# Sums of squares between the stages of a decoder trunk: VectorE adds the tiles and TensorE sums one

## What is computed

```python
def rmsnorm(x, g):
    xf = x.astype(jnp.float32)
    y = xf * lax.rsqrt(jnp.mean(xf * xf, axis=-1, keepdims=True) + EPS)
    return (y * g.astype(jnp.float32)).astype(x.dtype)
...
        hp = hp + rmsnorm(yp, g_post_mix[i])          # yp: the token mixer of rmsnorm(hp, g_pre_mix[i])
        fp, cvp = conv_ffn(rmsnorm(hp, g_pre_ffn[i]), ffn_w_up[i], ffn_conv_w[i], ffn_conv_b[i], ffn_w_down[i], ...)
        hp = hp + rmsnorm(fp, g_post_ffn[i])
        hp = hp + ple_term(hp, p_prompt[i], g_ple[i], ple_w_gate[i], ple_w_proj[i])
```

## Time and profile before

| what | before |
|---|---|
| device time, median of 3 runs | 1294.07 us |
| the profiled execution's own time | 1293.96 us |
| its span, first to last instruction | 1292.2 us |
| TensorE matmul busy | 1283.7 us (99%) |
| TensorE weight load busy | 1251.8 us (97%) |
| VectorE busy | 877.2 us (68%) |
| ScalarE busy | 593.1 us (46%) |
| GpSimd busy | 74.8 us (6%) |
| granted TensorE clock | 1.000 of full speed |

### The profile page before, as it was taken

How to read it: one execution, slowest core, us unless ns; L and a number is a source line. 1 busy time by engine, 2 the same in 40 slices (tenths; PEclk the granted TensorE clock), 3 DMA queues, 4 the chain that set the end, 5 groups by cost and what they waited for, 6 DMA issues and landing times.

```text
span 1292.2 us, 25278 instructions
## 1 busy us (share of the span) xinstructions
PE 1283.7 (99%) x10762; PEld 1251.8 (97%) x10762; DVE 877.2 (68%) x1656; ACT 593.1 (46%) x1060; POOL 74.8 (6%) x114
## 2 busy tenths in 40 slices
PE   9999999999999999999999999999999999999998
PEld 8999989999999999999999977999999999999998
DVE  7899776887777774223896788688777777422375
ACT  6214565544444443223755777554444444222371
POOL 1112230000100000000031020000000000000000
PEclk9999999999999999999999999999999999999999
DMA  5435621213342233222314232311332323322231
GB/s 197 155 102 192 201 98 51 99 66 104 96 107 85 96 106 119 90 90 78 132 53 159 66 99 81 115 50 52 96 94 87 98 84 109 114 90 91 78 131 67
DMA packets 35617, 131.85 MB, mean 102 GB/s; under 512 B 4516, under 2 KB 5260, under 8 KB 35184
## 3 DMA queue, kind: packets, MB, share of 16 engines
q1 hardware_dynamic: 29664, 111.33, 27.0%
q0 software_dynamic: 5408, 18.26, 4.4%
q10 hardware_dynamic: 432, 0.64, 0.2%
HBM read 121.26 MB, written 10.08 MB: 102 GB/s over the span
## 4 chain that ended last, share of the span: by engine, by line
PE 98%; DVE 1%; ACT 0%; DMA 0%; issue 0%; ACTq 0%; DVEq 0%
PE tile L1171 24%; PE tile L1175 24%; PE tile L1173 24%; PE tile L1181 5%; PE tile L1182 5%; PE tile L1183 5%; PE side L1181 1%; PE side L1182 1%; PE side L1183 1%; PE tile L1643 1%; PE side L1666 1%; PE sums L1220 0%; DMA raw<-in_w_kv 0%; PE sums L1681 0%; PE sums L1342 0%; PE sums L1688 0%
## 5 line engine op out<-in xcount | busy, mean ns | idle before, releaser
L749 ACT ACTIVATE wH<-raw 128x1024 fp32r<-128x1024 f32 (+1 forms) x190 | 211.0, 1114 | 384.9 <-DMA raw<-in_w_up 150.8
L1171 PE MATMUL tile<-xH,wH 128*128 128x260 f32 x1798 | 362.5, 283 | 0.0
L1175 PE MATMUL tile<-xH,wL 128*128 128x260 f32 x1798 | 362.4, 283 | 0.0
L1173 PE MATMUL tile<-xL,wH 128*128 128x260 f32 x1798 | 361.8, 283 | 0.0
L1813 DVE TENSOR_TENSOR wL<-raw,wH 128x1024 fp32r<-128x1024 f32 (+1 forms) x190 | 245.3, 1292 | 154.4 <-ACT wH L749 150.3
L1171 PEld LDWEIGHTS tile<-xH,wH 128*128 128x128 f32 x1798 | 277.1, 188 | 3.0 <-issue 3.0
L1175 PEld LDWEIGHTS tile<-xH,wL 128*128 128x128 f32 x1798 | 277.2, 188 | 0.0
L1173 PEld LDWEIGHTS tile<-xL,wH 128*128 128x128 f32 x1798 | 276.4, 188 | 0.0
L1873 DVE SCALAR_TENSOR_TENSOR u<-tile,rstd 128x520 f32<-128x520 f32 x96 | 67.1, 699 | 121.6 <-PE tile L1175 121.6
L1171 PE MATMUL tile<-hidH,wH 128*128 128x260 f32 x616 | 124.3, 283 | 0.0
L1175 PE MATMUL tile<-hidH,wL 128*128 128x260 f32 x616 | 123.8, 282 | 0.0
(11 more groups left out here) (434 smaller groups left out, 1878.7 us busy)
## 6 DMA issues: line engine op xcount, KB each, us to landing
raw<-in_w_up SPq DMA_DIRECT2D x88, 512.0 KB, 3.6
raw<-in_w_down SPq DMA_DIRECT2D x32, 704.0 KB, 4.1
raw<-in_w_ple SPq DMA_DIRECT2D x16, 512.0 KB, 6.5
raw<-in_w_qo SPq DMA_DIRECT2D x12, 512.0 KB, 3.7
raw<-in_w_qkv SPq DMA_DIRECT2D x12, 512.0 KB, 3.6
raw<-in_w_kv SPq DMA_DIRECT2D x10, 512.0 KB, 3.7
cring<-in_c_in POOLq DMA_DIRECT2D x8, 512.0 KB, 4.8
out_c_s<-cring POOLq DMA_DIRECT2D x8, 512.0 KB, 3.1
```

The lines of the kernel that those rows point to most:

```text
L749: nc.scalar.activation(wH[j][:, 0:n], raw[j][:, 0:n], ACT.Copy).then_inc(s_high, 1)
L1171: nc.tensor.matmul(out[:, q, 0:HT], wh, x[0][:, k, tokens(q)], start=first, stop=False)
L1173: nc.tensor.matmul(out[:, q, 0:HT], wh, x[1][:, k, tokens(q)], start=False, stop=False)
L1175: mm = nc.tensor.matmul(out[:, q, 0:HT], wl, x[0][:, k, tokens(q)], start=False, stop=last)
```

## The change

TensorE's column groups and ScalarE's copies of the group sums go. VectorE folds the squares of all four (stage, half) pairs of a layer, and TensorE sums one tile each. VectorE also adds the last unit of `y`'s second half to `acc`, so `y_sum` is one matmul everywhere. ScalarE applies the norm's gain when it copies `y`, and VectorE's first instruction of a `step` becomes a plain product of two tensors.

```diff
-            def square_group(stage, q, part):
-                pe.wait_ge(s_sq, SQ0[stage] + KT * q + 4 * part + 4)
-                if part == 0:
-                    pe.wait_ge(s_root, ROOT[POST[stage], q])
-                for j in range(4):
-                    mm = nc.tensor.matmul(sums[32 * j:32 * j + 32, q, 0:HT], ones[:, 0:32], square(stage, q, 4 * part + j),
...
             def square_sum(stage, q):
-                if (stage, q) in GROUPED:
-                    pe.wait_ge(s_psumr, GROUPED[stage, q])
-                else:
-                    pe.wait_ge(s_root, ROOT[POST[stage], q])
-                    pe.wait_ge(s_fold, int(stage[2]) + 1)
+                pe.wait_ge(s_root, ROOT[POST[stage], q])
+                pe.wait_ge(s_fold, FOLDED[stage, q])
...
-                first_half(up, 0, (s_yr, y0 + (15 if layer else 13)),
-                           lambda k: y_sum(mixer, 1) if k == 1 else square_sum(up, 0) if k == 3 else None)
+                def norm_sums(k):
+                    if k == 3:
+                        y_sum(mixer, 1)
+                        square_sum(up, 0)
+                first_half(up, 0, (s_yr, y0 + (15 if layer else 13)), norm_sums)
...
-                for k in range(4):
+                for k in range(6):
                     for c in range(SPLIT):
                         second_half(up, c, k, k + 1)
-                square_group(up, 1, 0)
-                square_group(up, 1, 1)
-                for c in range(2):
-                    second_half(up, c, 4, 5)
                 square_sum(up, 1)
...
                     for q in range(2):
+                        if j == 1 and q == 1:
+                            pe.wait_ge(s_yr, YREAD0[down] + KT + 1)
...
-                    if j == 0:
+                    if j == 1:
                         y_sum(down, 1)
-                    if j == 5:
-                        square_group(ple, 0, 0)
-                        square_group(ple, 0, 1)
...
                 for k in range(3):
                     for c in range(SPLIT):
                         second_half(ple, c, k, k + 1)
+                square_sum(ple, 0)
+                for k in range(3, 6):
+                    for c in range(SPLIT):
+                        second_half(ple, c, k, k + 1)
                 square_sum(ple, 1)
...
-                nc.scalar.activation(y[:, k, tokens(q)], src, ACT.Copy)
+                nc.scalar.activation(y[:, k, tokens(q)], src, ACT.Copy, scale=gains[:, layer, norm, k:k + 1])
...
-                        nc.vector.scalar_tensor_tensor(
-                            out=update(k), in0=y[:, k, tokens(q)], scalar=gains[:, layer, g_post, k:k + 1],
-                            in1=cg[:, tokens(q)], op0=ALU.mult, op1=ALU.mult).then_inc(s_update, 1)
+                        nc.vector.tensor_tensor(update(k), y[:, k, tokens(q)], cg[:, tokens(q)], ALU.mult
+                                                ).then_inc(s_update, 1)
...
-                fold_squares(up, 0)
+                fold_squares(up, 0, lambda: add_unit(mixer, KT - 1, 1))
...
                 for k in range(KT + 2):
                     step(k, 1)
+                fold_squares(up, 1)
                 pre_one_over(up, 0)
...
                 for k in range(KT + 2):
                     step(k, 0)
+                    if k == 5:
+                        dve.wait_ge(s_yr, YREAD0[down] + KT + 1)
+                        dve.wait_ge(s_acc, ACC0[down] + KT + 1)
+                        nc.vector.tensor_tensor(acc[:, tokens(1)], acc[:, tokens(1)], sq[:, (KT - 1) % 2, tokens(1)], ALU.add
...
-                one_over(down, 1, cg[:, tokens(1)], rstd[:, tokens(1)])
+                    if k == 7:
+                        one_over(down, 1, cg[:, tokens(1)], rstd[:, tokens(1)])
                 for k in range(KT + 2):
                     step(k, 1)
-                    if k in (1, 3, 4):
-                        low(ple, {1: 0, 3: 1, 4: 2}[k])
+                    if k in (0, 2, 3):
+                        low(ple, {0: 0, 2: 1, 3: 2}[k])
+                    if 4 <= k < KT:
+                        fold_embedding_squares(ple, k - 4)
+                    if k == KT:
+                        fold_late_squares(ple, 0)
...
+                fold_late_squares(ple, 1)
                 pre_one_over(ple, 0)
```

More of the change, by code:

```diff
@@ L765, in pre_root @@
                 nc.scalar.activation(rstd[:, tokens(q)], sums[:, q, 0:HT], ACT.Sqrt, bias=eps[:, 0:1],
-                                     scale=1.0 / (32 * D if (stage, q) in GROUPED else D)).then_inc(s_rootp, 1)
-            def group_sums(stage, q):
-                act.wait_ge(s_psum, GROUPED[stage, q])
-                nc.scalar.activation(square(stage, q, 0), sums[:, q, 0:HT], ACT.Copy).then_inc(s_psumr, 1)
+                                     scale=1.0 / D).then_inc(s_rootp, 1)
             def inputs(stage, k, q, layer, norm):
@@ L982, in feed_forward @@
                         src = bank(down, k)[:, :, 0:HT]
-                        nc.scalar.activation(halves(y_down[:, k, :]), src, ACT.Copy)
+                        nc.scalar.activation(halves(y_down[:, k, :]), src, ACT.Copy,
+                                             scale=gains[:, layer, G_POST_FFN, k:k + 1])
                         if k >= 2:
@@ L999, in ple_input @@
                     inputs(ple, k, q, layer, G_PLE)
-                y_unit(down, y_down, KT - 1, 0)
+                y_unit(down, y_down, KT - 1, 0, layer, G_POST_FFN)
                 root(down, 0, cg)
@@ L1242, in y_sum @@
                         pe.wait_ge(s_rootp, PREROOT["up" + stage[4], 1])
-                mm = nc.tensor.matmul(sums[:, q, 0:HT], ones, acc[:, tokens(q)], start=True, stop=whole)
-                if whole:
-                    mm.then_inc(s_ss, 1)
-                    return
-                pe.wait_ge(s_yr, YREAD0[stage] + (KT * (q + 1) if stage[:4] != "down" else KT + q))
-                nc.tensor.matmul(sums[:, q, 0:HT], ones, sq[:, (KT - 1) % 2, tokens(q)], start=False, stop=True
-                                 ).then_inc(s_ss, 1)
+                nc.tensor.matmul(sums[:, q, 0:HT], ones, acc[:, tokens(q)], start=True, stop=True).then_inc(s_ss, 1)
             X = (xH, xL)
@@ L1841, in fold_squares, with fold_embedding_squares, fold_late_squares @@
                     chain.link(nc.vector.tensor_tensor(tiles[:, 0:n, :], tiles[:, 0:n, :], tiles[:, n:2 * n, :], ALU.add))
+                between()
+                nc.vector.tensor_tensor(tiles[:, 0, :], tiles[:, 0, :], tiles[:, 1, :], ALU.add).then_inc(s_fold, 1)
+            def fold_embedding_squares(stage, part):
+                half = KT // 4
+                tiles = square(stage, 0, 0), square(stage, 0, 1)
+                if part < 2:
+                    early, late = sg[part], squares_ple[:, half * part:half * part + half, :].rearrange("p k t -> p (k t)")
+                    dve.wait_ge(s_sq, SQ0[stage] + KT)
+                    chain.did(nc.vector.tensor_tensor(early, early, late, ALU.add))
+                    return
+                dve.wait_ge(s_dve, chain.n)
+                if part == 2:
+                    chain.did(nc.vector.tensor_tensor(sg[0], sg[0], sg[1], ALU.add))
+                else:
+                    nc.vector.tensor_tensor(tiles[0], tiles[0], tiles[1], ALU.add).then_inc(s_fold, 1)
+            def fold_late_squares(stage, part):
+                tiles = squares_ple[:, KT // 2:KT // 2 + KT, :]
+                dve.wait_ge(s_sq, SQ0[stage] + KT + (KT // 2 if part == 0 else KT))
+                if part == 0:
+                    chain.did(nc.vector.tensor_tensor(tiles[:, 0:2, :], tiles[:, 0:2, :], tiles[:, 2:4, :], ALU.add))
+                    return
+                chain.link(nc.vector.tensor_tensor(tiles[:, 4:6, :], tiles[:, 4:6, :], tiles[:, 6:8, :], ALU.add))
+                chain.link(nc.vector.tensor_tensor(tiles[:, 0:2, :], tiles[:, 0:2, :], tiles[:, 4:6, :], ALU.add))
                 nc.vector.tensor_tensor(tiles[:, 0, :], tiles[:, 0, :], tiles[:, 1, :], ALU.add).then_inc(s_fold, 1)
@@ L2300, in feed_forward @@
                                         ).then_inc(s_acc, 1)
-                step = residual(down, ple, y_down, layer, G_POST_FFN, G_PLE)
+                step = residual(down, ple, y_down, layer, G_PLE)
                 one_over(down, 0, cg[:, tokens(0)], rstd[:, tokens(0)])
```

66 lines of the change are left out of this document (26 added, 40 removed).

## The result

| what | before | after |
|---|---|---|
| device time, median | 1294.07 us | 1299.21 us |
| ratio of after to before | | 1.0036, 95% interval 1.0025 to 1.0046 |
| five executions of after | | 1297.59, 1297.71, 1299.21, 1299.32, 1299.54 us |
| the profiled execution's own time | 1293.96 us | 1297.59 us |
| its span | 1292.2 us | 1295.8 us |

The change costs 5.1 us where 2.8 were forecast. The five executions fall into two groups: two of them near 1297.6, with a mean granted clock of 1.000, and three near 1299.3 at 0.998 to 0.999. The profiled execution belongs to the first group and shows a loss of 3.6 us; the rest of the median's loss, some 1.6, has a cause that this execution does not show.

A forecast was written before the change was run, and what follows sets the result against it. The prediction took TensorE, busy 99%, to set the time until it meets unfinished VectorE or ScalarE work. Net losses of 0.75 (`up`) and 0.65 (`ple`) per layer, 2.8 in all, gave 1296.9 us, range 1295.2 to 1298.4.

The forecast's parts named there:

- the sum: Both layers together: 2 x (0.75 in `up` + 0.65 in `ple`) = 2.8 us slower.
- What goes away on TensorE: Per layer three column groups of 1.21 and two second sums of 0.43 go: 8.98 us for both layers.
- Step 1: `up`: the second half's `y_sum` waits 0.02 for VectorE's add; the root and VectorE's second half begin 0.31 later.
- Step 2: `up`: eight VectorE steps cost 0.34 instead of 0.41, so the last `xL` starts about 0.23 earlier, at 243.36.
- Steps 3 to 5: `up`: a fold of 2.34 uses up VectorE's slack; chunk 3 waits until 251.08, chunk 5 starts 0.75 later.
- Step 6: `pw`: ScalarE's copy of tile 4 comes later, so TensorE waits 1.1 and starts tile 6 at 624.87.
- steps 7 and 8: `ple`: the root holds the last `xH`, then fold and reads follow; chunk 3 starts at 648.26, 0.65 later per layer.
- A: Rival: VectorE's work is covered everywhere and TensorE gives back all that is taken from it: 1285.1 us, chance 0.07.
- B: Rival: only `up` waits; `ple` is covered if its last `xH` starts before 638.6: 1289.9 us, chance 0.08.
- C: Rival: only `ple` waits, `up`'s fold overlapping something counted in series: 1292.1 us, chance 0.08.
- D: Rival: VectorE's lag behind `ple` reaches layer 1's first tiles, 0.5 to 1.5 more: about 1298 us, chance 0.07.

The follow-up runs named there:

- fill: The changed kernel with products without use on TensorE ahead of its four new waits, 41 more per layer: 1297.81 us.
- up_groups_fill3: The changed kernel with `up`'s second half back to column groups and 15 useless products ahead of chunk 3 of `ple`: median 1295.95 us.
- y_only: The changed kernel with `up`'s second half and both halves of `ple` back to column groups, keeping the moved y sums and the gain in ScalarE's copy: 1293.03 us.
- copy_early: The changed kernel with ScalarE's copy of `pw` tile 4 moved ahead of the last `xH` of the first half: 1297.90 us.
- root_late: The changed kernel with ScalarE's root of `ple`'s first half moved behind the last `xH` of the second half: 1293.92 us.
- ple_groups: The changed kernel with both halves of `ple` back to column groups and the root of its first half back in its old place: 1295.58 us.
- gpsimd_folds: The changed kernel with the folds of `up`'s second half and of `ple` on GpSimd, `pw` tile 4 copied early and `ple`'s first sum moved: 1296.83 us.

## Why the prediction was wrong

The direction was right (slower, 0.49), and every wait that it named is there; the time lies 0.7 us above the top of the range. Point by point:

- **The step that failed: the sum.** It counts each wait at its length and puts at nothing what a standstill costs besides. Three of five executions took some 1.6 longer than the two others, and the median with them; with the standstills filled (*fill*) none of six did. With `up` in column groups, it is the standstill of 2.0 at chunk 3 of `ple` that does it (*up_groups_fill3*). Four waits were forecast, and none was asked what TensorE's clock does behind it. Without this term the time would have been 1297.6, inside the range: 3.6 more in an undisturbed execution against the 2.8 forecast. Of those 0.8, `up` has about 0.7 (1.05 in layer 0 and 1.18 in layer 1 against 0.75 twice) and `ple` next to nothing (0.71 and 0.58 against 0.65 twice).
- **What goes away on TensorE.** Forecast 8.98 if nothing waited. The second sums, 0.43 each, are mis-sized: taken alone (*y_only*) four of them bring 1.06 instead of 1.72, because the new sum meets VectorE's add and loses 0.18.
- **Step 1 failed in size.** It had the sum wait 0.02 and take 0.60. The sum loses 0.18, 0.07 ahead of it and 0.11 within it (it takes 0.71), and ScalarE's root starts at 233.00 instead of 232.88.
- **Step 2 failed.** The products do cost 0.34 from start to start. But the last `xL`, forecast 0.23 earlier than before (0.56 less 0.31 is 0.25), comes 0.07 later (243.66 against 243.59), with the same 0.18 of waiting for `xH` ahead of it as in the earlier trace rows: VectorE begins the half 0.42 later and wins back 0.35 of it and not 0.56, since at that place ScalarE sets the pace, and a faster VectorE only waits. The step took the sum of the gains and did not look at who stood beside it.
- **Steps 3 to 5 hold, the chunks 0.2 late.** The fold takes 2.35, the slack of 0.95 is gone, chunk 3 starts at 251.28 (forecast 251.08) and chunk 5 at 263.47 (263.27). `down`, behind `up`, starts 1.05 later in layer 0 (488.47 against 487.42), against 0.75.
- **Step 6 holds.** `up`'s delay had put `pw` 1.05 later; without it, tile 6 starts at 624.89, forecast 624.87. That this wait is handed on to chunk 3, as steps 7 and 8 have it, agrees with *copy_early*, where 0.2 less of waiting ahead of the sum made chunk 3 start 0.2 earlier.
- **Steps 7 and 8 hold.** Without the same 1.05, the root starts at 640.39 (640.24), the last `xH` at 640.76 (640.6), chunk 3 at 648.32 (648.26), 0.71 later than before against 0.65. *root_late* shows that the place of the root is the cause.
- **The rivals.** A is refuted by the two waits at chunk 3. B is not what happened, but its condition was the right one: with the last `xH` early (*root_late*) `ple`'s long wait goes. B's 1289.9 left out tile 6's wait, which then counts. C is refuted by *ple_groups*. D is not needed: the parts add up without it.

## What to carry to other kernels

An engine that is 99% busy gives back what is taken from it only up to the next read, copy or root that it meets; before moving work to the other engines, write down for each such meeting point how much slack there is, and who sets the pace there. Where a moved step leaves a new wait, look at the order of the one queue that releases it: here one ScalarE instruction, moved by one place, was worth as much as the whole loss. And where an engine comes to stand still for about 2 us, look at several executions and not only at the profiled one: here such a standstill could cost more than its length in one stage and did not in another, and filling it with useless products was faster than waiting.

## What the runs showed of the hardware

- A TensorE standstill of 2.0 us in `ple` went with executions up to 3.5 us longer at mean granted clocks down to 0.997: 4 of 7 and 6 of 10 executions lay above 1296.47 us, and none of 10 with it filled with products. One of 1.9 in `up` went with no such spread in 20.
- While GpSimd added two tiles in SBUF (1.31 us for 520 columns), VectorE's operations with two tensors in SBUF stood: 1.54 us for one that takes 0.42 (*gpsimd_folds*).
- A scale from a tile, one value per partition, adds 0.09 us to ScalarE's copy of 260 columns from PSUM (0.48; the same copy without it took 0.39 in the kernel before), where the prediction had 0.08. ScalarE's timeline of the changed kernel, copy of the last unit:

```profile
230.93 0.48 ACT L788 ACTIVATE y_ml<-tile,front 128x260 f32<-128x260 f32 x1 [2.12 <-PE tile L1174]
```
